# A streaming encoder layer on one core: half stores, later waits, and a sum moved from VectorE to GpSimd in twenty attention groups

## The reference

```python
(aq, ak, av, iq, ik, iw, za, uv, zb, glu, zc, gates) = split_columns(rms_norm(x, norm_g) @ w_in)
# A: each query keeps the 256 best visible keys of a lightning indexer, then
#    softmax attention over them with ALiBi, 8 heads of 64, 2 kv heads
# B: gMLP: gelu, LayerNorm(v), 128x128 chunk-causal mixing
# C: GLU, causal depthwise conv of width 31, LayerNorm, swish
merged = (ga * ((o_a * silu(za)) @ w_a) + gb * ((o_b * silu(zb)) @ w_b) + gc * ((o_c * silu(zc)) @ w_c))
x = x + merged @ w_out
x = x + sigmoid(rms_norm(x, ple_g) @ w_pg) * (p @ w_ple)
y = rms_norm(x, final_norm_g)
```

## Time and profile before

| | us |
|---|---|
| median of 3 runs (lowest, highest) | 2663.24 (2659.4, 2665.63) |
| the profiled execution's own time | 2664.84 |
| its span, first to last instruction | 2663.0 |

### The profile page before, as it was taken

The page is one execution under the profiler, slowest core; times in us unless marked ns, Lnnn a source line. Parts: engine busy times, 40 slices in busy tenths (PEclk is TensorE's granted clock), DMA queues, the critical chain, the costliest instruction groups (busy, mean ns, idle before and its releaser), DMA issues. The chain is left out here.

```text
span 2663.0 us, 40101 instructions
## 1 busy us (share of the span) xinstructions
PE 2598.4 (98%) x13799; PEld 2411.6 (91%) x13799; DVE 2056.7 (77%) x3877; ACT 1501.8 (56%) x2550; POOL 1490.0 (56%) x1074
## 2 busy tenths in 40 slices
PE   8999999999999999999999979999999999999998
PEld 8999999999999999999999967777889999877886
DVE  6377899999999999996462478999976567657656
ACT  5377578687877777775212377777760101325553
POOL 1100188687868786798344566321247563976562
PEclk9999999999999999999999989999999999999999
DMA  4433323233433332223465653222148875742221
GB/s 180 132 117 123 127 94 126 89 123 109 136 99 122 99 123 96 91 91 130 158 205 164 184 146 101 76 62 68 54 138 307 326 273 195 245 162 99 89 91 56
DMA packets 279880, 359.95 MB, mean 135 GB/s; under 512 B 37825, under 2 KB 227905, under 8 KB 279037
## 3 DMA queue, kind: packets, MB, share of 16 engines
q1 hardware_dynamic: 171667, 219.73, 25.9%
q10 hardware_dynamic: 108010, 137.66, 14.9%
HBM read 216.94 MB, written 139.74 MB: 134 GB/s over the span
## 5 line engine op out<-in xcount | busy, mean ns | idle before, releaser
L1761 PE MATMUL psum<-hT_hi,j_whi 128*128 128x416 f32 x2432 | 865.0, 356 | 3.5 <-ACT j_out L1600 2.7
L1761 PE MATMUL psum<-hT_hi,j_wlo 128*128 128x416 f32 x2432 | 852.8, 351 | 0.0
L1761 PE MATMUL psum<-hT_lo,j_whi 128*128 128x416 f32 x2432 | 851.6, 350 | 0.0
L1313 POOL TENSOR_TENSOR v_y<-v_y,v_product 128x422 f32<-128x422 f32 x459 | 559.1, 1260 | 82.3 <-ACT v_product L1295 82.3
L449 DVE TENSOR_SCALAR_CACHE_REDUCE s_tie<-s_key,s_bits 128x640 bf16<-128x640 f32 (+14 forms) x352 | 464.2, 1319 | 12.3
L1761 PEld LDWEIGHTS psum<-hT_hi,j_whi 128*128 128x128 f32 x2432 | 456.2, 188 | 13.4 <-ACT j_out L1600 3.5
L1761 PEld LDWEIGHTS psum<-hT_lo,j_whi 128*128 128x128 f32 x2432 | 457.4, 188 | 9.1 <-issue 1.6
L1761 PEld LDWEIGHTS psum<-hT_hi,j_wlo 128*128 128x128 f32 x2432 | 456.2, 188 | 5.5
L1295 ACT ACTIVATE v_product<-v_x,v_taps 128x422 f32<-128x422 f32 x510 | 305.0, 642 | 111.4 <-POOL v_y L1313 89.5
L1520 POOL TENSOR_TENSOR j_wlo<-j_w,j_whi 128x1024 fp32r<-128x1024 f32 x59 | 145.0, 2457 | 310.8 <-ACT j_whi L1580 310.8
L1600 ACT ACTIVATE j_out<-psum 128x416 f32<-128x416 f32 x285 | 144.5, 508 | 295.2 <-PE psum L1761 283.9
(11 more groups left out here) (369 smaller groups left out, 4907.8 us busy)
## 6 DMA issues: line engine op xcount, KB each, us to landing
T_dram<-j_out ACTq DMA_DIRECT2D x58, 624.0 KB, 3.0
j_w<-in_w_in ACTq DMA_DIRECT2D x59, 512.0 KB, 3.8
T_dram<-j_out ACTq DMA_DIRECT2D x60, 416.0 KB, 2.4
m_gate<-T_dram SPq DMA_DIRECT2D x60, 416.0 KB, 4.7
m_oraw<-B_dram SPq DMA_DIRECT2D x15, 832.0 KB, 6.7
M_dram<-m_merged ACTq DMA_DIRECT2D x5, 1664.0 KB, 10.9
n_x<-in_x_prompt SPq DMA_DIRECT2D x16, 512.0 KB, 6.1
G_dram<-f_prepsums ACTq DMA_DIRECT2D x8, 1024.0 KB, 5.9
```

Source lines behind the costliest of these rows:

```text
L1313: pool.tensor_tensor(y[k % 2][:], y[k % 2][:], product[n % RING][:], ALU.add).then_inc(added, 1)
L1761: last = pe.matmul(bank, w[p][:, k, :], h[:, k, t0:t0 + SPAN], start=(k == 0 and q == 0), stop=(k == KD - 1 and q == 2))
```

## The change

Five edits. (1) In SyncE's list the load and the move of the last shared convolution unit go ahead of the move of VectorE's last own unit (`AFTER_LAST_OWN`). (2) The last of the five diagonal products of the LayerNorm stands three slices later on TensorE. (3) The transposes of a group's first key tile wait for the exponential of each head, one head at a time, instead of for all four. (4) For groups 10 to 29 ScalarE copies all 128 partitions of the bank (`a_oraw`, in the place of `a_olow`), VectorE does nothing, and GpSimd adds the two halves in two instructions; TensorE waits for the copy instead of for `po_read`. (5) `m_merged` is stored in two halves of four blocks, each with its own semaphore.

```diff
-        upcoming = [0]
+        upcoming, AFTER_LAST_OWN = [0], 28
...
-            units(SELECT_US + us)
+            units(SELECT_US + us + (AFTER_LAST_OWN if what == "unit" and t + 1 == len(OWN) else 0))
...
-    STEP, SQUARES, SPREAD = 28, 15, 27
+    STEP, SQUARES = 28, 15
+    SPREAD_AT = [STEP * x + 27 + 3 * (x == X - 1) for x in range(X)]
...
+        def sum_halves(group):
+            o = of_group(oa, group)
+            pool.wait_ge(o_copied, group.n + 1)
+            pool.wait_ge(stored[group.p], group.m * 16)
+            pool.tensor_tensor(o, o_raw[HD:P], c.zero[HD:P].to_broadcast([HD, 512]), ALU.add).then_inc(o_moved, 1)
+            pool.wait_ge(o_moved, SUMMED_BY_GPSIMD.index(group.n) + 1)
+            pool.tensor_tensor(o, o_raw[0:HD], o, ALU.add).then_inc(po_read[group.g], 1)
...
+            if group.n - 1 in SUMMED_BY_GPSIMD:
+                sum_halves(groups[group.n - 1])
             if group.n:
                 gate(groups[group.n - 1])
                 end(groups[group.n - 1])
...
+    SUMMED_BY_GPSIMD = range(LATE_GROUPS.stop, last_prompt.n - 1)
...
-            if x == 0:
-                pe.wait_ge(exp_done, group.exponentials_before + len(group.buffers))
...
             for r, (h, block) in enumerate((h, block) for h in group.buffers for block in group.blocks(kt)):
+                if x == 0 and block == group.blocks(kt)[0]:
+                    pe.wait_ge(exp_done, group.exponentials_before + group.buffers.index(h) + 1)
...
-            if x == 0 and group.i:
+            if x == 0 and group.n - KVH in SUMMED_BY_GPSIMD:
+                pe.wait_ge(o_copied, group.n - KVH + 1)
+            elif x == 0 and group.i:
                 pe.wait_ge(po_read[g], group.i)
...
+            if group.n in SUMMED_BY_GPSIMD:
+                act.activation(o_raw[:], c.psum[:, PO[group.g], :], ACT.Copy).then_inc(o_copied, 1)
+                return
...
         def finish(group):
+            if group.n in SUMMED_BY_GPSIMD:
+                return
...
+        def store_half(span, half):
+            blocks = slice(4 * half, 4 * half + 4)
+            act.wait_ge(added, 16 * span + 12 + 4 * half)
+            act.dma_start(c.M_dram[blocks, :, span * SPAN:(span + 1) * SPAN].rearrange("s q t -> q s t"), merged[:, blocks, :]
+                          ).then_inc(stored[half], 16)
...
+                if z == 1:
+                    store_half(0, 0)
                 c.store_sums(act, z)
+                if z == 1:
+                    store_half(0, 1)
...
-            act.wait_ge(added, 16 * (span + 1))
-            act.dma_start(c.M_dram[:, :, span * SPAN:(span + 1) * SPAN].rearrange("s q t -> q s t"), merged[:]).then_inc(stored, 16)
+            if span:
+                store_half(span, 0)
+                store_half(span, 1)
...
-                    vec.wait_ge(stored, 16 * span)
+                    vec.wait_ge(stored[n // 4], 16 * span)
```

More of the change, by code:

```diff
@@ L951, in tensor_in @@
             turn_tails(pe)
-        if n >= SPREAD and (n - SPREAD) % STEP == 0 and (n - SPREAD) // STEP < X:
-            x = (n - SPREAD) // STEP
+        if n in SPREAD_AT:
+            x = SPREAD_AT.index(n)
             pe.wait_ge(diagonal_full, x + 1)
@@ L1975, in stage_attend @@
     oa = [sb(f"a_oa{p}", [HD, HEADS, P]) for p in range(2)]
-    o_low = sb("a_olow", [HD, 512])
+    o_raw = sb("a_oraw", [P, 512])
+    o_low = o_raw[0:HD]
     factor = [sb(f"a_factor{g}", [HD, 512]) for g in range(KVH)]
@@ L2007, in stage_attend @@
     rs_cleared, rs_made = S("a_rs_cleared"), S("a_rs_made")
-    exp_done, rs_ready, pt_full, pt_hi, o_copied, factor_made = (
-        S("a_" + n) for n in ("exp_done", "rs_ready", "pt_full", "pt_hi", "o_copied", "factor_made"))
+    exp_done, rs_ready, pt_full, pt_hi, o_copied, factor_made, o_moved = (
+        S("a_" + n) for n in ("exp_done", "rs_ready", "pt_full", "pt_hi", "o_copied", "factor_made", "o_moved"))
     pt_free = [S(f"a_pt_free{u}") for u in range(RING)]
@@ L2486, in finish @@
                 act.wait_ge(po_read[1 - group.g], group.i + group.g)
-            act.activation(by_head(group, o_low[:]), by_head(group, c.psum[HD:P, PO[group.g], :]), ACT.Copy).then_inc(o_copied, 1)
+            if group.n in SUMMED_BY_GPSIMD:
+                act.activation(o_raw[:], c.psum[:, PO[group.g], :], ACT.Copy).then_inc(o_copied, 1)
+                return
+            act.activation(by_head(group, o_low), by_head(group, c.psum[HD:P, PO[group.g], :]), ACT.Copy).then_inc(o_copied, 1)
         in_order(Actions(start=start, first=first, head=head, turned=turned, weigh=weigh, finish=finish, end=end))
@@ L2591, in finish @@
                 vec.wait_ge(stored[group.p], group.m * 16)
-            vec.tensor_tensor(of_group(oa, group), by_head(group, c.psum[0:HD, PO[group.g], :]), by_head(group, o_low[:]), ALU.add
+            vec.tensor_tensor(of_group(oa, group), by_head(group, c.psum[0:HD, PO[group.g], :]), by_head(group, o_low), ALU.add
                               ).then_inc(po_read[group.g], 1)
@@ L2669, in stage_merge @@
     g_full = [S(f"m_g_full{x}") for x in range(4)]
-    product, gated, added, stored = S("m_product"), S("m_gated"), S("m_added"), S("m_stored")
+    product, gated, added = S("m_product"), S("m_gated"), S("m_added")
+    stored = [S(f"m_stored{half}") for half in range(2)]
     hi_done, lo_done = S("m_w_hi"), S("m_w_lo")
@@ L2803, in vector @@
                     low(2, n // 2)
-    c.merged_stored = lambda eng, span=len(SPANS) - 1: eng.wait_ge(stored, 16 * (span + 1))
+    c.merged_stored = lambda eng, span=len(SPANS) - 1: [eng.wait_ge(half, 16 * (span + 1)) for half in stored]
     c.merged_products = lambda eng, s=LAST: eng.wait_ge(product, 8 * s + 8)
```

## The result

The changed kernel takes 2643.50 us (median of 4 executions, 2642.72 to 2651.85) against 2663.36 us of the kernel before: ratio 0.9937, 95% interval 0.9920 to 0.9954, so 20 us less. The forecast was 2645. The execution under the profiler took 2642.72 us, 22.1 less than the profiled one of before.

The account below looks back on a forecast made before the run. TensorE was taken as the bound, busy 2598.4 of 2663.0 us, so only its idle time could be won. Terms 1.8 + 1.4 + 2.5 + 7 + 4.3 + 2.1 = 19.1 us gave 2645 us, range 2634 to 2656.

Parts of the forecast that it names:

- The mechanism: Last shared unit: loads go before the own unit's wait, so GpSimd, ScalarE's copy and TensorE stop waiting; 1.8 us.
- 12.2 us of idle time: TensorE's idle time in attention, 1640 to 1955 us; set 12 as upper end for the GpSimd sum, 7 taken.
- TensorE's wait for `a_ptlo` halved: Sign in attention groups 12 to 30: TensorE's wait for VectorE's `a_ptlo` halves, while VectorE's waits for products get longer.
- the first rival: Attention: TensorE takes up VectorE's place, so the GpSimd sum gives 0 to 2 instead of 7 us; 2651, chance 0.15.
- ScalarE's queue: Merge: rival that this queue or full DMA engines hold the first half store past 2053.9, gap stays; 2651, chance 0.05.
- The clock term: Behind the merge gap: without it the clock should stay at 2.4 GHz; 2.3 us, ends 0 and 2.3, 2.1 taken.
- The slower rival: Attention: GpSimd late with `po_read` holds up ScalarE's next copy, then TensorE; 2674, or 2671 by the variant; chance 0.05.
- 2.4 us of room: Group 11: GpSimd's halves done at 1634.1, ScalarE wants `a_oraw` at 1636.51; tightest place for GpSimd's lateness.
- the variant: Attention: GpSimd's extra 2.6 us per group stretches one VectorE instruction by 1.3 us; twenty groups cost 26 us, 2671.
- term 2: Last LayerNorm diagonal: three more slices ahead of it on TensorE remove its wait for VectorE; 1.4 us, ends 0 and 1.4.
- terms 1, 4 and 5: SyncE's order 1.8 us; twenty groups summed on GpSimd 7 us; half stores in the merge 4.3 us plus clock 2.1.
- terms 1, 3 and 5: SyncE's order 1.8 us; transposes one head at a time 2.5 us; half stores in the merge 4.3 us plus clock 2.1.

Follow-up runs that it names:

- slow sum: Changed kernel with GpSimd doing the first of its two group-sum instructions seven times in all twenty groups; 2664.78 us, ratio 1.0005.
- three more groups: Changed kernel with groups 0, 1 and 30 also summed by GpSimd; 2651.02 us, ratio 0.9957 to the kernel before.

## Why the prediction was right

**Edit 1** (forecast 1.8). The mechanism is as told. The size fits where the wait was there: group 0 starts about 2.2 us earlier than in the kernel before. One profile without the edit (1540.9) shows that the loss of 1.84 us in the earlier trace rows was not in every execution; there the same wait of GpSimd was 8.44 us and the copy for TensorE came in time. By time alone the edit is not shown (2.3 us for edits 1 and 2, with an interval that holds 0).

**Edit 2** (forecast 1.4): wrong, it gives nothing. I had written that the swish behind the diagonal has "1.4 us less to the start of attention" and priced that at zero. That was the next wait: 0.68 us for `a_lows` at 1536.42 in the trace of before already said that VectorE was late there. With the edit this wait is 2.0 to 3.0 us in eight profiles, and 0.4 to 0.8 in the six without it.

**Edit 3** (forecast 2.5): 2.3 us in groups 11 to 33 (1.3 to 3.1), and the wait went from 8.0 to 3.6. What it gives in groups 0 to 11 lies under their scatter.

**Edit 4** (forecast 7 of at most 12): 8.0 us in its stretch, and 10.1 as the median. The step behind its size does not hold as told: I took the 12.2 us of idle time as the ceiling of what could come back, and two fifths of the gain came from elsewhere. Cut to the same work, groups 11 to 33, the kernel before, the one with edit 4 alone, and the changed one (edits 3 and 4 together):

```profile
1626.50:1977.70 351.20, 335.14 (x1952) 274.50 (x1951) 325.51 (x823) 270.18 (x427) 111.10 (x77) 1.00 0.25 75
```
```profile
1626.30:1969.40 343.10, 331.93 (x1952) 276.16 (x1951) 315.87 (x802) 265.26 (x426) 156.94 (x117) 1.00 0.25 76
```
```profile
1622.10:1963.20 341.10, 330.25 (x1952) 275.19 (x1951) 315.99 (x803) 265.35 (x427) 157.00 (x117) 1.00 0.26 77
```

For the same 1952 matmuls edit 4 alone took off 4.9 us of idle time (16.06 to 11.17) and 3.2 us of busy time; both edits took off 5.2 and 4.9. The matmuls themselves hardly became shorter (a transposition takes 275 ns on average in the first two kernels). What shrank is in the main, as I read it, time that the rows hide because they overlap. One place in the kernel before shows how:

```profile
1648.77 0.39 PE L2404 MATMUL psum<-a_khi,a_qs 128*128 128x512 f32 x1
1649.00 0.39 PE L2405 MATMUL psum<-a_klo,a_qs 128*128 128x512 f32 x1
1649.42 0.63 PE L2361 MATMUL psum<-ident,a_l 128*128 128x128 f32 x4
```
```profile
1649.39 0.42 PEld L2361 LDWEIGHTS psum<-ident,a_l 128*128 128x128 f32 x4 [0.43 <-DVE a_ptlo L2553]
```

The second product starts 0.23 us behind the first and is shown for 0.39. The weight load behind it waits 0.43 us for `a_ptlo`, so the transpositions start 0.42 us behind the second product, and yet the matmul rows show no idle time. It is the wait of the weight loads that tells of it. Between 1640 and 1955 us it was 27.5 us in the earlier trace rows, and in the changed kernel it is 20.7:

```profile
PEld psum L2374 <- DVE a_ptlo L2571: 20.7, 37, 1.1
...
PE psum L2374 <- DVE a_ptlo L2571: 6.9, 19, 0.7
```

So "TensorE's wait for `a_ptlo` halved" did not come true (10.4 to 6.9), and yet the gain did. VectorE's waits for products did not grow (4.3 us to 1.9 between 1640 and 1955), which kept the first rival out.

**Edit 5** (forecast 4.3 and 2.1): 6.8 us in the stretch against the kernel before, 4.4 to 6.5 against three others, 7.6 in the median. ScalarE's queue held nothing up: with edit 5 alone the first half went out at 2035.26, where I had put it at 2035.8. The clock term is the uncertain one, 0.9 to 2.9 us by these kernels.

**The slower rival.** GpSimd's lateness is real and has the place that I gave, group 11: 0.26 us. The slow sum shows its price, a microsecond of TensorE for each one that ScalarE waits, and that my 2.4 us of room was for a single group; the backlog decides. Contention, the variant, has next to no share in these groups: `a_ptlo` takes 683 ns without the sum on GpSimd and 685 in every kernel with it, with GpSimd busy for 134 us or for 247. What looks like it stood only where VectorE's two inputs were in SBUF, with group 30 added.

Sum by the runs: 2.2 + 0 + 2.3 + 8.0 + 6.8 = 19.3, against 19.1 forecast and 19.9 measured. That it fits so closely is in part luck. The too large term 2 (1.4 for nothing) and the too small terms 1, 4 and 5 (0.4, 1.0 and 0.4) offset one another. And terms 1, 3 and 5 of this sum are read against one profile of the kernel before, and each moves by about 2 us with the profile that is chosen.

## What to carry to other kernels

Compare two traces between marks in the work, not between clock times: the same count of matmuls in fewer microseconds is the gain, and 40% of it (3.2 of 8.1 us here) may sit in time that counts as busy. Ahead of taking a wait away, look at the next place where the same two engines meet; a short wait there (0.68 us here) means that the win is only moved. Work that goes to an engine with much idle time costs nothing until a neighbouring short group, or a list that follows it, finds that engine late; then it costs about one for one (20.6 us of waits, 21.3 us of time), and lateness carries over groups.

## What the runs showed of the hardware

GpSimd's addition of a zero to partitions 64 to 127, written to partitions 0 to 63, took 1038 ns, less than its addition of two inputs on partitions 0 to 63 (1287 ns); my price had been 1289 for both. ScalarE's copy from PSUM took 591 ns for 128 partitions and 594 for 64, with 512 columns in both.

TensorE's gap of 4.30 us cost 2.5 us more than itself in the merge, and gaps of 3.49 to 3.62 us cost 0.9 to 2.9 more; behind or beside each of them the granted clock fell (to 0.50, the lower level of 1.2 GHz, in the lowest stretch of 5 us). With the gap closed it stayed at 1.00 (2.4 GHz), and so it did around a gap of 1.86 us. That agrees in kind with what the Trainium skill says of the clock (page "TensorE: Matmul & The Clock Gate", section "What's actually happening"), that throttled is the default state and activity releases it.

I had not expected contention between VectorE and GpSimd to decide a run, and in the kernel with three more groups it seems to have done so, though no run tried it by itself: a GpSimd product of 1.27 us took 3.78 beside VectorE's subtractions of two SBUF inputs, and of four such subtractions two were slower as well. Beside `a_ptlo`, which has one input in PSUM, GpSimd's 64x512 product kept its 1.28 to 1.29 us, and `a_ptlo` its 685 ns, with GpSimd busy for 134 us and for 247. Both agree with the rule that I had cited from the Trainium skill (page "SBUF — State Buffer", section "Who interferes with whom"): a VectorE instruction contends with GpSimd's reads when it has two SBUF inputs. The section names one more case, VectorE's 2-port modes, which the prediction left out; it says that `tensor_tensor`, the instruction of these rows, has none.
